# Second feed-forward matrix: four pairs of seven block products, with weight sums made by accumulating transfers

## The reference, cut to what matters

```
def _squared_relu_mlp(h, w1, w2):
    return jnp.square(jax.nn.relu(h @ w1)) @ w2      # h 512 x 1024, w1 1024 x 4096, w2 4096 x 1024
...
x = x + _rms_norm(ffn, norm_ffn_post)                # and then the norm ahead of the next layer
```

## Time and profile before

| | us |
|---|---|
| median of three runs | 1752.04 |
| profiled execution, its own time | 1751.83 |
| its span | 1750.1 |
| PE busy in the span | 1720.5 (98%) |
| DVE busy | 1058.1 (60%) |
| ACT busy | 869.3 (50%) |
| POOL busy | 367.2 (21%) |
| a pair of seven products (1086.7 to 1124.7) | 38.0 |
| layer 0, after the last pair to the end of the last down unit | about 65.3 |

### The profile page before, as it was taken

One profiled execution on the slowest core, in us unless ns is written; L12 is line 12 of the kernel. 1 busy time (PEld: TensorE's weight loads), 2 busy tenths in 40 slices (PEclk: granted clock), 3 DMA queues, 4 the chain that ended last, 5 costly groups with the idle time before them and its releaser, 6 DMA issues.

```text
span 1750.1 us, 21182 instructions
## 1 busy us (share of the span) xinstructions
PE 1720.5 (98%) x8319; PEld 1376.0 (79%) x8319; DVE 1058.1 (60%) x1408; ACT 869.3 (50%) x1410; POOL 367.2 (21%) x197
## 2 busy tenths in 40 slices
PE   7999999999999999999999999999999999999998
PEld 5888777778787767876988888888876798888886
DVE  6611567685976367954467576745457247686855
ACT  4324566557635353254563535336677356354542
POOL 0443322123244233433400000004410330000000
PEclk9999999999999999999999999999999999999999
DMA  8524322221132322311232231322320241414031
GB/s 314 209 92 120 97 61 60 74 73 55 67 121 80 109 73 72 108 49 57 91 131 100 93 128 65 121 73 64 96 66 1 97 145 48 147 47 169 25 130 75
DMA packets 83935, 166.25 MB, mean 95 GB/s; under 512 B 6041, under 2 KB 8222, under 8 KB 83838
## 3 DMA queue, kind: packets, MB, share of 16 engines
q1 hardware_dynamic: 83838, 164.93, 28.3%
HBM read 157.64 MB, written 2.10 MB: 91 GB/s over the span
## 4 chain that ended last, share of the span: by engine, by line
PE 92%; DVE 4%; ACT 2%; issue 1%; POOL 1%; DMA 0%; SPq 0%; DVEq 0%; ACTq 0%; POOLq 0%
PE PDT L779 10%; PE PDT L781 10%; PE PDT L780 10%; PE PDT L768 9%; PE PDT L770 8%; PE PDT L769 8%; PE PM L970 4%; PE PM L965 4%; PE PM L963 4%; PE PM L1153 2%; PE PM L1427 2%; PE PDT L1388 2%; PE PM L1388 2%; PE PM L1120 1%; PE PM L1180 1%
## 5 line engine op out<-in xcount | busy, mean ns | idle before, releaser
L2201 POOL TENSOR_TENSOR wlo<-wraw,whi 128x512 fp32r<-128x512 f32 (+5 forms) x112 | 324.2, 2911 | 933.6 <-ACT whi L1589 758.8
L779 PE MATMUL PDT<-hhi,whi 128*128 128x512 f32 x796 | 312.3, 392 | 0.5 <-POOL wlo L2201 0.5
L781 PE MATMUL PDT<-hhi,wlo 128*128 128x512 f32 x796 | 310.2, 390 | 0.0
L780 PE MATMUL PDT<-hlo,whi 128*128 128x512 f32 x796 | 310.1, 390 | 0.0
L1705 ACT ACTIVATE whi<-wraw 128x2048 fp32r<-128x2048 f32 x78 | 149.5, 1917 | 276.1 <-PE PM L970 120.5
L2876 DVE TENSOR_TENSOR wlo<-wraw,whi 128x2048 fp32r<-128x2048 f32 x78 | 178.7, 2291 | 160.9 <-ACT whi L1705 160.7
L768 PE MATMUL PDT<-whi,hhi 128*128 128x512 f32 (+1 forms) x592 | 233.4, 394 | 1.1 <-DVE hlo L2611 0.6
L770 PE MATMUL PDT<-whi,hlo 128*128 128x512 f32 (+1 forms) x592 | 227.9, 385 | 0.0
L769 PE MATMUL PDT<-wlo,hhi 128*128 128x512 f32 (+1 forms) x592 | 227.8, 385 | 0.0
L1589 ACT ACTIVATE whi<-wraw 128x2048 fp32r<-128x2048 f32 (+3 forms) x71 | 129.3, 1821 | 173.7 <-PE PDT L770 75.8
L779 PEld LDWEIGHTS PDT<-hhi,whi 128*128 128x128 f32 x796 | 149.5, 188 | 31.5 <-issue 1.5
(11 more groups left out here) (409 smaller groups left out, 2873.5 us busy)
## 6 DMA issues: line engine op xcount, KB each, us to landing
wraw<-in_mlp_w SPq DMA_DIRECT2D x64, 1024.0 KB, 5.1
wraw<-in_w_in SPq DMA_DIRECT2D x26, 1024.0 KB, 5.1
wraw<-in_even_w_in SPq DMA_DIRECT2D x16, 1024.0 KB, 5.2
w_ada<-in_w_ada SPq DMA_DIRECT2D x11, 1024.0 KB, 12.9
wraw<-in_w_out SPq DMA_DIRECT2D x8, 1024.0 KB, 4.9
swapped<-qk_sb SPq DMA_DIRECT2D x16, 256.0 KB, 7.2
wraw<-in_even_w_out SPq DMA_DIRECT2D x4, 1024.0 KB, 4.9
wraw<-in_odd_w_o SPq DMA_DIRECT2D x4, 1024.0 KB, 4.9
```

Source lines behind the costliest of these rows:

```text
L779: mm(bank, sth, hi[:, k0 + k, :], start=start and k == 0, stop=False)
L780: mm(bank, sth, lo[:, k0 + k, :], start=False, stop=False)
L781: last = mm(bank, stl, hi[:, k0 + k, :], start=False, stop=stop and k == 3)
L2201: part = g.tensor_tensor(wlo[base % 2][:, cols], wraw[base % 2][:, cols], fl(whi[base % 2][:, cols]), ALU.subtract)
```

## The change

Chunks 6 and 7 become a fourth pair of seven products. So the second matrix takes 4 x 7 units of 24 matmuls in a layer, and a layer has 44 weight units instead of 41. `up(7)` is moved ahead of the third pair's products: PE's order now ends with `up(6), up(7), products(2), products(3)`, and the fourth pair has no `up` between it and the third.

The weight sums are no longer made by DVE. A block is loaded into a raw slot, and POOL issues a transfer that adds another block from HBM to what lies in the slot (`accum_op`). There are five of these for a pair, 1 MB each, and each waits until the one before has landed (`w_added`). Within a pair the products now come in the order P1, P2, P6, P5, P7, P3, P4; in the fourth P3 and P7 change places (`turn_of`), and its products other than P3 use the banks PDT.

The parts of the fourth pair need the places of the third's, so ACT and DVE make them between the third pair's weight splits, each once the product that held the place is used up (`late_high` on ACT, `late_sum` and `late_low` on DVE).

At the end the four tiles are not alike: tiles 0 and 1 are complete after P3 and before P4, tiles 2 and 3 with P4 (step F). `mh_hi`, `mh_lo` and step G are gone, `mixr` lies elsewhere in the arena, the arena starts at a multiple of 64 bytes, and the scratch for descriptors is 2048 instead of 1024.

```
-MLP_UNITS = 41
-CHUNKS = [0, 2, 4, 13, 15, 24, 26, 35]
-PAIRED = [6, 17, 28]
+MLP_UNITS = 44
+CHUNKS = [0, 2, 4, 13, 15, 24, 26, 28]
+PAIRED = [6, 17, 30, 37]
+P1, P2, P6, P5, P7, P3, P4 = range(7)
...
+SUMMED = {P6: ("e", 2), P7: ("b", 3), P5: (P1, 4), P4: ("e", 5)}
...
-    MIX1_ORDER = ["F0", "F1", "G0", "M0", "F2", "X0", "G1", "M1", "B0", "F3", "X1", "G2", "B1", "C0", "M2", "C1",
-                  "G3", "X2", "M3", "X3", "B2", "B3", "C2", "C3"]
-    LAST_ORDER = ["F0", "F1", "G0", "M0", "F2", "X0", "G1", "M1", "F3", "X1", "G2", "M2", "G3", "X2", "M3", "X3"]
+    MIX1_ORDER = ["M0", "X0", "M1", "B0", "X1", "B1", "C0", "C1", "F2", "M2", "F3", "M3", "X2", "X3", "B2", "B3", "C2",
+                  "C3"]
+    LAST_ORDER = ["M0", "X0", "M1", "X1", "F2", "M2", "F3", "M3", "X2", "X3"]
...
+            after, d = d, PAIRED[3]                       # SP
+            split(after + P5)
+            down((u0 + d, "e"), 6, 0)
+            split(after + P7)
+            down(u0 + d + P1, 6, 0)
+            split(after + P3)
+            down(u0 + d + P2, 7, 0)
+            split(after + P4)
+            down((u0 + d, "b"), 6, 1)
+            split(d + P2)
+            down(u0 + d + turn_of(3, P3), 7, 1)
...
+                    high(0)                               # PE, product
+                    if p == 3 and n in (P3, P4):
+                        unit_wait(u)
+                        low(0).then_inc(S(f"bank_full{(P3, P4).index(n)}"), 1)
+                        if n == P4 and after is not None:
+                            tile_transposes(after, 0, 1)
+                        high(1)
...
+                if p == 3:
+                    product(P1, 0, True, 0)
+                    product(P2, 1, True, 0)
+                    product(P6, 0, False, base + 1)
+                    product(P5, 1, True, base + 2)
+                    product(P3, 1, True, 0)
+                    product(P7, 0, False, base + 3)
+                    product(P4, 0, False, base + 8)
+                    return
...
+            up(6)
+            up(7)
+            products(2)
+            products(3)
...
+            for n in range(7):                            # ACT
+                raw_hi(PAIRED[2] + n + 2)
+                for part in late.get(n, []):
+                    late_high(*part)
...
+            def added(key, c, h, count, after=None):      # POOL
+                slot, loaded = RAW[key]
+                if count > 1:
+                    pool.wait_ge(S("w_added"), 16 * (count - 1))
+                pool.wait_ge(S(f"w_loaded{slot}"), loaded)
+                if after is not None:
+                    pool.wait_ge(S("w_split"), u0 + after + 1)
+                g.dma_start(wview(wraw[slot], 4, 512), w2_v[layer][:, 4 * c:4 * c + 4, 512 * h:512 * h + 512],
+                            accum_op=ALU.add).then_inc(S("w_added"), 16)
+
+            for p, d in enumerate(PAIRED):
+                c, n = 2 * p, 20 * layer + 5 * p
+                added((u0 + d, "e"), c, 1, n + 1)
+                added((u0 + d, "e"), c + 1, 1, n + 2)
+                added((u0 + d, "b"), c + 1, 1, n + 3)
+                added(u0 + d + P1, c, 1, n + 4, d + P1)
+                added((u0 + d, "e"), c + 1, 0, n + 5, d + P6)
...
-                add_raw(a, c, u0 + o + P3)                # DVE
-                gather(p, P1, 0, 0, 0, ALU.add, -3)
-                add_raw(b, c, u0 + o + P3)
```

More of the change, by code:

```diff
@@ L306, in build_program @@
     mixm = arena("mixm", [P, TT, DM], 56)
-    mixr = arena("mixr", [P, TT, DM], 72)
+    mixr = arena("mixr", [P, TT, DM], 16)
     kva = arena("kva", [P, TT, 288], 16)
@@ L966, in product, with low @@
                                skip_group_check=True)
[L967 to L968 removed]
+                    def low(t):
                         for k in range(4):
@@ L971, in product @@
                                       skip_group_check=True)
-                    last.then_inc(S("w_used"), 1)
-                pe.wait_ge(S("part_made"), 6 * layer + 2 * p + 2)
+                        return last
+                    pe.wait_ge(S("w_hi"), u + 1)
+                    high(0)
[5 more added lines that the diff above has]
+                        high(1)
+                    else:
+                        high(1)
+                        unit_wait(u)
+                        low(0)
@@ L977, in products @@
                 product(P6, 0, False, base + 1)
-                product(P2, 1, True, base + 3)
-                product(P7, 0, False, base + 4)
+                product(P5, 1, True, base + 2)
+                product(P7, 0, False, base + 3)
                 product(P3, 1, True, base + 5)
                 product(P4, 0, False, base + 6)
[L983 to L1012, removed]
             first_up()
             up(1)
-            for p in range(3):
+            for p in range(2):
                 up(2 * p + 2)
@@ new lines, in late_sum @@
+            def late_sum(m, n, first, second):
+                dve.wait_ge(S("hid_made"), 32 * layer + 32)
+                dve.wait_ge(S("w_used"), u0 + PAIRED[2] + n + 1)
+                for g in range(2):
+                    a, b, o = first(g), second(g), part_sum[n][:, 2 * g:2 * g + 2, :]
+                    if m in (1, 3):
+                        dve.wait_ge(S("part_summed"), 32 * layer + 24 + (g + 1 if m == 1 else 3 + g))
+                        op = v.scalar_tensor_tensor(out=o, in0=a, scalar=-1.0, in1=b, op0=ALU.mult, op1=ALU.subtract)
+                    else:
+                        op = v.tensor_tensor(o, a, b, ALU.subtract)
+                    op.then_inc(S("part_summed"), 1)
@@ new lines, in late_low, with a11 @@
+            def late_low(n, high, source=None):
+                for g in range(2):
+                    whole = part_sum[n][:, 2 * g:2 * g + 2, :] if source is None else source(g)
+                    dve.wait_ge(S("part_high"), 56 * layer + 42 + 2 * high + g + 1)
+                    op = v.tensor_tensor(part_lo[n][:, 2 * g:2 * g + 2, :], whole, fl(part_hi[n][:, 2 * g:2 * g + 2, :]),
+                                         ALU.subtract)
+                op.then_inc(S("part_made"), 1)
+            def a11(g):
+                return hid_a[:, 2 * g:2 * g + 2, 0:2 * P]
```

316 lines of the change are left out of this document (179 added, 137 removed), and 3 rows, old and new, of the table MLP_LOADS.

## The result

The changed kernel takes 1780.12 us (median of 4 runs, 1777.77 to 1782.78) against 1751.95 (4 runs, 1751.81 to 1753.19): ratio 1.0158, 95% interval 1.0146 to 1.017. It is slower, by 28 us where 5 were forecast, and outside the range.

A forecast was written before the change was run, and what follows sets the result against it. PE, busy 98% of the span, was taken as the bound. The terms -10.9 + 5.8 + 2.8 + 4.6 + 1.4 + 1.6 = +5.3 on 1751.83 gave 1757.1, forecast as 1757 us; range 1747 to 1775.

The forecast's parts named there:

- 1 matmuls: On PE's path, 24 fewer matmuls a layer at 0.2267 us each: -10.9 us for two layers.
- 2 P1, P2, P6 late: Fourth pair: DVE and ACT work moved between the third pair's products makes PE wait, 2.9 us a layer, +5.8.
- 3 P7, then P4: Fourth pair: both on side 0 with nothing between, so P4 waits 1.4 us for P7's gather; +2.8 for both layers.
- 4 end of layer 0: PE waits of 2.9, 0.8 and 2.1 us around tile turns and bank 0, less 1.2 before: +4.6.
- 5 end of layer 1: x is complete 6.0 us behind PE's end instead of 4.6: +1.4.
- 6 adding transfers: Fourth pair: at 8.6 us an add, P5's sum comes 0.8 us late; +1.6 for both layers.
- The path of all four adds: Fourth pair: P5's sum ready no sooner than block "e" landed at 20.5 us plus four adds.
- The other path: Fourth pair: block "b" lands at 38.9 us, then two adds; at 8.6 each P5's sum is ready at 56.1.
- The threshold of 55.3: Fourth pair: when ACT wants P5's sum, 2.0 us before PE wants P5 at 57.3; adds up to 8.2 cost nothing.
- The rival of long adds: Adds take 10 to 13 us, PE stands at the fourth pair's P5; 1766 at 10, about 1785 at 12; chance 0.25.
- a landing over 9.3: Sign in POOL's adding transfers that the forecast is wrong; it expected 8 to 9 us to landing.
- the 0 for the new start of the arena: Arena's new start, with the scratch and moved `mixr`: no instruction changes its length by a row at hand; 0 us.

The follow-up runs named there:

- e2_no_adds: The changed kernel with all 40 adding transfers left out, a small memset in their place, weights not summed; 1759.43 us, ratio 1.0041.
- e1_swap: The changed kernel with the fourth pair's third and fourth adding transfers exchanged, P5's sum ahead of P7's; 1769.5 us, ratio 1.0098.
- e8_all: The changed kernel with two fourth-pair sums per layer on DVE, late ACT and DVE work reordered, tile 0's transposes later, arena at a multiple of 512; 1751.98 us.
- e11_before_shifted: The kernel before the change with only the arena's start moved, 448 bytes behind a multiple of 512; 1754.39 us, ratio 1.0016.
- e3_plain: The changed kernel with the same 40 transfers from POOL's queue overwriting instead of accumulating, weights not summed; 1758.58 us, ratio 1.0043.
- e4_align: The changed kernel with the arena at a multiple of 512 bytes again and descriptor scratch 1536 instead of 2048; 1782.34 us, ratio 1.0164.
- e9_layer_end: e8_all with layer 0's end reordered on DVE and ACT, P3's gathers ahead of P4's weight split; 1748.4 us, ratio 0.998.

## Why the prediction was wrong

| step | predicted, us | measured, us | from |
|---|---|---|---|
| 1 matmuls | -10.9 | -10.9 | 48 fewer |
| 2 P1, P2, P6 late | +5.8 | +3.7 | 2 x (0.34 + 0.25 + 1.27) |
| 3 P7, then P4 | +2.8 | +2.7 | 2 x 1.36 |
| 4 end of layer 0 | +4.6 | +4.1 | waits of 7.3 now, 3.2 before |
| 5 end of layer 1 | +1.4 | +1.1 | 8.5 against 7.4 |
| 6 adding transfers | +1.6 | +17.1 | 8.46 + 8.61 |
| clock | 0 | +5.6 | half of 11.1 us |
| matmul pitch | 0 | +3.0 | 1344 x 0.0022 |
| sum | +5.3 | +26.4 | spans: +28.1 |

1.7 us aren't placed.

Steps 1 to 5 held in place and size, apart from step 2, whose collisions cost two thirds of what was worked out. The step that failed is 6, by its constants: 8.6 us for an add and 5.1 for a load, wherever they stand. Undisturbed both are nearly right (8.4 to 8.8 for most adds, and 4.9 to 5.3 for the loads of this stretch in e2_no_adds). But 5.1 was read in a trace in which the engines were at 0.31, and 8.6 was worked out from it, and both were used in a stretch that the change itself fills to 0.87. The path of all four adds, 20.5 + 4A, which gives 54.9 for an A of 8.6, is the one that decided:

| from the third pair's start at 1108.7 | predicted, us | measured, us |
|---|---|---|
| P5's split ends | 15.4 | 15.5 |
| block "e" landed | 20.5 | 22.9 |
| four adds, each behind the one before | 34.4 | 39.4 |
| between landings and issues | 0 | 1.8 |
| P5's sum ready | 54.9 | 64.1 |

The other path, "b is loaded behind P4's (33.7) and lands at 38.9", was taken for the later one, at 56.1. Its split ended at 33.9 and the block landed at 43.0, 4.1 late, but the second add landed at 44.7, and only then could the third start. The threshold of 55.3 stayed: 64.1 is 8.8 late, of which PE saw 8.5. The prediction had the numbers, 6.0 us of the engines for an add and 3.0 for a load. It added up landings along a chain and never asked what lands beside them on the same engines: 37.5 us of their time in 41.2.

The rival of long adds named the place and the mechanism. The four adds took 9.85 each in the mean, next to its case of 10 (1766). What it held against itself, "only 0.31 of the queues are in use", is the premise that failed. The rest of the way to 1780 is the first block, the gaps, the clock and the pitch. The test "a landing over 9.3" did fire: 14 of the 40 adds are over it, the longest 11.9, and only their median, 8.7, hides it.

Two terms were missing. The clock: behind a long wait of PE half of what it does at 1.2 GHz is lost as well; in e1_swap and e8_all too a half clock stands behind the waits. The pitch: the 0 for the new start of the arena was an argument from silence. That the diff moved `A0` from 512 to 64 was there to see, and e11_before_shifted prices it at 2.5 us in the old kernel.

Of the two pages weighed: the half rate of reducing transfers is what the runs show (e3_plain). That POOL's issues leave DVE's additions alone (the Trainium skill, SBUF — State Buffer, "SBUF: two separate sides") agrees with the trace in the one form that it has: a split beside the issue at 1153.71 took 2.29 us, as without one.

## What to carry to other kernels

A transfer that saves an engine work is paid in the DMA engines' time; add that up over the stretch in which it happens, loads included, before chaining landings, because landings measured at a share of 0.31 didn't hold at 0.87. Count for every wait of PE what the granted clock takes behind it. And treat a moved start address as part of the change.

## What the runs showed that was not expected

- An accumulating transfer of 1 MB (fp32, from HBM into SBUF, issued by POOL) takes 5.9 us of the 16 engines for a million bytes, 1.30 us of POOL and mostly 8.4 to 8.8 us to land with nearly no load beside it, up to 11.9 with loads; the overwriting one 2.9, 0.76 and 5.5 (median).
- A load of a weight unit beside such transfers took up to 9.4 us in the fourth pair of layer 0 and 10.6 in layer 1; without them, 4.9 to 5.3 (e2_no_adds).
- The chain of waits can name the wrong transfer where an instruction waits for two: it put the third add's start down to the load of "b", 2.0 us before the landing that it stood behind.
- With the start of the arena 448 bytes behind a multiple of 512, a matmul of 512 columns whose loaded tile (`part_hi`, `part_lo`) lies there takes 0.2289 us instead of 0.2267, 1.0% (e4_align, e11_before_shifted). Other offsets weren't tried.
- After a wait of 8.5 us the granted clock was 0.50 for 3.3 and 4.4 us of work; behind the short waits close together at layer 0's end it was so too (3.4 us), and in e9_layer_end, with waits of up to 1.6, it stayed at 1.
